# Attention's products of weights and values: fp32 products of 65 columns, or fp32r products of split operands, 130 and 66 columns wide

## The chip, the cores and the metric

The kernel runs on one core of one Trainium2 chip. The time is that of the device from the start to the end of one execution, in microseconds (us); lower is better. The core has five engines that run on their own and meet at semaphores: TensorE (PE in the rows; its weight loads are listed as PEld), VectorE (DVE), ScalarE (ACT), GpSimd (POOL) and SyncE (SP), which here only issues DMAs.

## The reference, cut to what matters

One decoder layer over 1024 tokens of width 1024, all in float32: a projection, two groups of attention heads, an output projection, a mixture of experts, a gated input embedding and a final norm. The change lies in attention alone. Group A has 8 heads with three branches each (keys of all earlier tokens, keys of the last 512 tokens, and 63 compressed keys), group B has 8 heads with a cumulative forget gate in the logits. Since there are just 16 blocks of 64 keys and 16 are selected, the selected branch is plain causal attention.

```python
def _masked_softmax(logits, mask):
    l = jnp.where(mask, logits.astype(jnp.float32), NEG_INF)
    return jax.nn.softmax(l, axis=-1) * mask
...
    # _nsa_mixer, for each block of 64 queries: three branches
    s_c = jnp.einsum('bqghd,bngd->bghqn', qg, kc) * scale
    p_c = _masked_softmax(s_c, cmp_end[None, :] <= t[:, None])
    o_c = jnp.einsum('bghqn,bngd->bqghd', p_c.astype(vc.dtype), vc)
    ...
    o_s = jnp.einsum('bghqk,bgqkd->bqghd', p_s.astype(v_sel.dtype), v_sel)
    ...
    o_w = jnp.einsum('bghqk,bkgd->bqghd', p_w.astype(v_w.dtype), v_w)
    o = gt[..., 0:1] * o_c + gt[..., 1:2] * o_s + gt[..., 2:3] * o_w
...
    # _fox_mixer, for each block of 128 queries
    logits = (jnp.einsum('bqhd,bkhd->bhqk', qb, k).astype(jnp.float32) * scale
              + (cq[..., None] - cum[:, :, None, :]))
    p = _masked_softmax(logits, kpos[None, :] <= t[:, None])
    o = jnp.einsum('bhqk,bkhd->bqhd', p.astype(v.dtype), v)
```

## The kernel before

The stages run one after another, each in a scope of its own: `stage_project`, `stage_compress`, `stage_attention`, `stage_mix`, `stage_route`, `stage_moe`, `stage_finish`. Only `stage_attention` (from L764) is touched.

Work in attention is cut into **units**: a head, a branch (CAUSAL, NEAR, BLOCKS or, for the forgetting heads, FOX) and a half of the queries (four tiles of 128). A unit's blocks of 128 x 128 scores are packed into **banks** of at most 512 columns (`BANKS`). An ordinary head has 20 banks (3 and 7 of CAUSAL, 3 and 5 of NEAR, 1 and 1 of BLOCKS), a forgetting head 10 (3 and 7). That makes 16 heads, 64 units and 240 banks, of which 200 are 512 columns wide and 40 are 256. The banks hold 8 x (36 + 30 + 8) + 8 x 36 = 880 blocks of 128 x 128, and each block takes one product of weights and values.

Scores are computed with the keys on the PSUM partitions, so that a block of exponentials can serve as the stationary operand of the product with the values. The softmax's shift must then be a row of the query operand. It is found ahead: for each head, `minimum` on TensorE computes the scores again, with the queries on the partitions (19 tiles of 512 columns for an ordinary head, 9 for a forgetting one), VectorE reduces each (L1223, L1227), `join` merges halves, `turn` transposes the result, ScalarE copies it (`rows_out`, L1170), and a DMA (L901) writes it into rows of `q_two`. PSUM has `MX` = 4 places for these tiles; a place is free again when VectorE has taken its tile (`ring_before`). `share` spreads the minima of head i + 1 over the banks of head i: over the first 15 of the 20 banks of an ordinary head whose successor is ordinary, over the first 5 of the 10 of a forgetting head (two in each of four banks, one in the fifth).

TensorE's order is a loop over banks b: the scores of bank b + 1 (`score`, L1085, L1096 and the masks L1105), the minima that fall to this bank (L1041, masks L1052), perhaps the turns (L1064), then `weigh(b)` (L1123). The values have a column of ones, so a product has 65 columns and the sum of the weights comes out as the 65th. Both operands of `weigh` are fp32; the other products of attention are fp32r, on operands split into a rounded part and a rest. ScalarE follows with one exponential for each bank (`exps`, L1178) into one of `PT` = 3 buffers. VectorE's order for bank b is its minima, then `leave(u)` if a unit ended with bank b - 1: a reciprocal of the sums (L1248), a product with the gate (L1252, ordinary heads), one with a constant for BLOCKS (L1255), and the output times that (L1259, or L1264 into `tmp` which GpSimd adds, L981). The output of a unit is in one PSUM bank of two, so the first product of unit u waits for `o_made`, that is for `leave(u - 2)`:

```python
                    pe.wait_ge(expd, b + 1)
                    if first_of_unit and u >= 2:
                        pe.wait_ge(o_made, u - 1)
...
                    for kb, qa, qb, at in parts:
                        for q in range(qa, qb):
```

GpSimd makes the rests of the queries and keys (L937, L947) and the additions. SyncE's queue holds the loads of a head, the copies of its rounded halves (`second`) and the row of minima (`rows`).

## Time and profile before

| | us |
|---|---|
| Three runs | 1594.08, 1595.18, 1598.6 (median 1595.18) |
| The profiled execution | 1597.06, of which the span from the first to the last instruction is 1595.4 |
| Attention's stretch, TensorE dense in it | 382.5 to 798 |
| Busy in the span | TensorE 1397.2, VectorE 760.9, ScalarE 629.0, GpSimd 148.5 |
| Mean granted TensorE clock | 0.941 |

The profile gives, for one execution, every instruction with its start and its length. A product's length covers its way through the engine, and products overlap; what one costs in a dense stretch is the distance from one start to the next. Of n equal instructions merged into one row, that distance is the row's length less that of one, divided by n - 1. The granted clock is 1.00 for 2.4 GHz and 0.50 for 1.2 GHz. In a row of windows the columns are the window, its length, busy time with count in brackets for PE, PEld, DVE, ACT and POOL, the granted clock, the DMA engines' share and GB/s.

### The profile page before, as it was taken

The numbers are of one execution on the slowest core, as the hardware profiler recorded it, in microseconds if no ns is written. First come the engines' busy times: TensorE is split into PE (matmuls) and PEld (weight loads), VectorE is DVE, ScalarE is ACT, GpSimd is POOL, SyncE is SP. The second block draws the span as 40 slices with busy tenths as digits, with TensorE's granted clock in tenths as the row PEclk, the third lists the DMA queues.
The fourth block names the chain that finished last, engine by engine and source line by source line (L and its number), as shares of the span: only waits on it lengthen the run. The fifth ranks groups of instructions, "written<-read, shape, count | busy, mean of one in ns | idle before, by whom it ended". The sixth has DMA issues, their size and how long they took to land. (4 is left out here: it accounts for less than half of the span.)

```text
span 1595.4 us, 24135 instructions
## 1 busy us (share of the span) xinstructions
PE 1397.2 (88%) x7996; PEld 1167.6 (73%) x7997; DVE 760.9 (48%) x1240; ACT 629.0 (39%) x930; POOL 148.5 (9%) x146
## 2 busy tenths in 40 slices
PE   4999999737999999999969964999999999628997
PEld 3777889735899989888858854777777777516774
DVE  6633012235444444434254235678654767626552
ACT  6211110013333333445443212567644657515442
POOL 0000000013111112322000000010000000011000
PEclk9999999967999999999979975999999999858999
DMA  5122321144000012354033215799877979464410
GB/s 185 55 75 93 118 75 35 36 104 97 21 21 22 21 46 57 81 125 93 12 121 115 83 53 203 285 331 389 315 253 243 375 259 377 180 237 158 137 49 39
DMA packets 107988, 222.48 MB, mean 139 GB/s; under 512 B 14749, under 2 KB 41405, under 8 KB 107910
## 3 DMA queue, kind: packets, MB, share of 16 engines
q1 hardware_dynamic: 96950, 183.07, 35.4%
q0 software_dynamic: 7488, 27.27, 4.8%
q10 hardware_dynamic: 3472, 11.09, 1.7%
q8 instruction: 50, 0.82, 0.2%
q14 instruction: 28, 0.23, 0.0%
HBM read 176.56 MB, written 36.24 MB: 133 GB/s over the span
## 5 line engine op out<-in xcount | busy, mean ns | idle before, releaser
L1178 ACT ACTIVATE att_prob<-att_ps_s 128x512 f32<-128x512 f32 (+1 forms) x240 | 134.7, 562 | 246.2 <-PE att_ps_s L1105 201.3
L1227 DVE TENSOR_REDUCE att_mx<-att_ps_m 128x1 f32<-128x512 f32 (+3 forms) x256 | 132.8, 560 | 135.0 <-PE att_ps_m L1052 123.2
L1924 DVE TENSOR_TENSOR moe_g_lo<-moe_g_raw,moe_g_hi 128x1024 fp32r<-128x1024 f32 x128 | 148.1, 1218 | 45.5 <-ACT moe_g_hi L1844 44.8
L135 PE MATMUL moe_ps_g<-moe_g_hi,moe_xT_hi 128*128 128x512 f32 x336 | 137.7, 410 | 17.8 <-DVE moe_g_lo L1924 17.7
L1844 ACT ACTIVATE moe_g_hi<-moe_g_raw 128x1024 fp32r<-128x1024 f32 x128 | 124.9, 1047 | 44.4 <-PE moe_ps_g L137 24.4
L1123 PE MATMUL att_ps_o<-tok_vsw,att_prob 128*128 128x65 f32 x1056 | 140.1, 274 | 0.0
L136 PE MATMUL moe_ps_g<-moe_g_lo,moe_xT_hi 128*128 128x512 f32 x336 | 134.3, 400 | 0.0
L137 PE MATMUL moe_ps_g<-moe_g_hi,moe_xT_lo 128*128 128x512 f32 x336 | 133.9, 399 | 0.0
L1123 PEld LDWEIGHTS att_ps_o<-tok_vsw,att_prob 128*128 128x128 f32 x1056 | 131.2, 192 | 2.6 <-ACT att_prob L1178 0.5
L135 PE MATMUL prj_ps_w<-prj_hT_hi,prj_w_hi 128*128 128x512 f32 x256 | 103.0, 402 | 3.0 <-DVE prj_w_lo L405 3.0
L136 PE MATMUL prj_ps_w<-prj_hT_lo,prj_w_hi 128*128 128x512 f32 x256 | 100.3, 392 | 0.0
L137 PE MATMUL prj_ps_w<-prj_hT_hi,prj_w_lo 128*128 128x512 f32 x256 | 100.3, 392 | 0.0
L135 PEld LDWEIGHTS moe_ps_g<-moe_g_hi,moe_xT_hi 128*128 128x128 f32 x336 | 64.0, 190 | 38.4 <-DVE moe_g_lo L1924 21.2
L1929 DVE TENSOR_TENSOR moe_d_lo<-moe_d_raw,moe_d_hi 128x1024 fp32r<-128x1024 f32 x64 | 74.0, 1217 | 23.0 <-ACT moe_d_hi L1850 23.0
L135 PE MATMUL moe_ps_y<-moe_d_hi,moe_hT_hi 128*128 128x512 f32 x168 | 69.2, 412 | 12.0 <-DVE moe_d_lo L1929 12.0
L1123 PE MATMUL att_ps_o<-tok_vb,att_prob 128*128 128x65 f32 x576 | 75.9, 273 | 0.0
L137 PEld LDWEIGHTS moe_ps_g<-moe_g_hi,moe_xT_lo 128*128 128x128 f32 x336 | 64.1, 191 | 15.6
L136 PEld LDWEIGHTS moe_ps_g<-moe_g_lo,moe_xT_hi 128*128 128x128 f32 x336 | 64.2, 191 | 13.8
L1123 PEld LDWEIGHTS att_ps_o<-tok_vb,att_prob 128*128 128x128 f32 x576 | 72.1, 192 | 1.9 <-ACT att_prob L1178 0.2
L338 ACT ACTIVATE att_w_out<-prj_ps_w 128x512 f32<-128x512 f32 x28 | 16.7, 598 | 140.4 <-PE prj_ps_w L137 140.4
L1850 ACT ACTIVATE moe_d_hi<-moe_d_raw 128x1024 fp32r<-128x1024 f32 x64 | 62.4, 1045 | 19.4 <-issue 19.4
L136 PE MATMUL moe_ps_y<-moe_d_lo,moe_hT_hi 128*128 128x512 f32 x168 | 67.1, 399 | 0.0
(339 smaller groups left out, 2909.8 us busy)
## 6 DMA issues: line engine op xcount, KB each, us to landing
moe_g_raw<-in_w_gate_e SPq DMA_DIRECT2D x128, 256.0 KB, 4.9
moe_g_raw<-in_w_up_e SPq DMA_DIRECT2D x128, 256.0 KB, 6.2
moe_d_raw<-in_w_down_e SPq DMA_DIRECT2D x64, 512.0 KB, 7.6
y_rows<-moe_y ACTq DMA_DIRECT2D x21, 512.0 KB, 6.1
prj_w_raw<-in_w_in SPq DMA_DIRECT2D x16, 512.0 KB, 4.0
att_q_raw<-feat SPq DMA_DIRECT2D x32, 256.0 KB
feat<-att_w_out POOLq DMA_DIRECT2D x14, 512.0 KB, 2.9
att_k_raw<-feat SPq DMA_DIRECT2D x24, 256.0 KB
```

Of the source, the lines that this page charges most:

```text
L135: nc.tensor.matmul(out, a_hi, b_hi, start=first, stop=False)
L136: nc.tensor.matmul(out, a_hi, b_lo, start=False, stop=False)
L137: return nc.tensor.matmul(out, a_lo, b_hi, start=False, stop=last)
L338: nc.scalar.activation(out[:, h * 512:(h + 1) * 512], ps_w[:, h, :], ACT.Copy, scale=scale).then_inc(evac, 1)
L1123: last = nc.tensor.matmul(ps_o[:, u % 2, (q % 4) * HV:(q % 4 + 1) * HV], prob[:, b % PT, at + (q - qa) * P:at + (q - qa + 1) * P], value(k ...
L1178: nc.scalar.activation(prob[:, b % PT, 0:w], ps_s[:, b % ST, 0:w], ACT.Exp, scale=-1.0).then_inc(expd, 1)
L1227: last = nc.vector.tensor_reduce(mx[i % 2][:, col, q:q + 1], p[:, at:at + (kb - ka) * P], X, ALU.min)
L1844: nc.scalar.activation(g_hi[:, ch % GR], g_raw[:, ch], ACT.Copy).then_inc(s_ghi, 1)
L1850: nc.scalar.activation(d_hi[:, ch % DR], d_raw[:, ch], ACT.Copy).then_inc(s_dhi, 1)
L1924: nc.vector.tensor_tensor(g_lo[:, ch % GR], g_raw[:, ch], g_hi[:, ch % GR].bitcast(F32), ALU.subtract).then_inc(s_glo, 1)
L1929: nc.vector.tensor_tensor(d_lo[:, ch % DR], d_raw[:, ch], d_hi[:, ch % DR].bitcast(F32), ALU.subtract).then_inc(s_dlo, 1)
```

## The change

The exponentials of a bank are computed twice from PSUM, once rounded to fp32r (`prob_hi`) and once in fp32 (`prob`), and VectorE subtracts the one from the other (`rest`) into `prob_lo`. GpSimd splits the values in the same way into `val`, where the rounded part and the rest of a block of keys lie side by side, 2 x 65 = 130 columns. A block of weights and values is then two fp32r products: `weigh(b, 0)`, the rounded weights times all 130 columns, and `weigh(b, 1)`, the rest of the weights times 66 columns (the rounded values, and one column beside them). The second runs one bank later, behind `weigh(b + 1, 0)`. A unit's output has two sums of 65 columns for each tile of queries and takes two PSUM banks; `leave` first adds the two (a reduction of 512 numbers to 256 into `kc_raw`), and does so one bank later than before. The minima have 2 places in PSUM instead of 4; there are 2 buffers of exponentials instead of 3, one `mT` instead of two, the row of minima goes in two DMAs, and `tmp` lies in `K["cos"]`, whose later load waits for the last addition.

```diff
-        QS, RAW, ST, MX, PT, TM = 3, 2, 2, 4, 3, 2
+        QS, RAW, ST, MX, PR, VR, TM = 3, 2, 2, 2, 2, 3, 2
...
-        prob = sc.sb("prob", [P, PT, 512])
+        prob = sc.sb("prob", [P, PR, 512])
+        prob_hi = sc.sb("prob_hi", [P, PR, 512], F32R)
+        prob_lo = sc.sb("prob_lo", [P, PR, 512], F32R)
+        val = [sc.sb(f"val{s}", [P, NT, 2, HV], F32R) for s in range(VR)]
+        val_c = sc.sb("val_c", [P, GROUPS, 2, HV], F32R)
         mx = [sc.sb(f"mx{s}", [P, 5, NT]) for s in range(2)]
-        mT = [sc.sb(f"mT{s}", [3, S], F32R) for s in range(2)]
+        mT = sc.sb("mT", [3, 2, 512], F32R)
         wt = sc.sb("wt", [P, 2, 4])
-        tmp = sc.sb("tmp", [P, TM, 4, HD])
+        tmp = K["cos"][:, 0:TM * 4 * HD].rearrange("p (a q d) -> p a q d", a=TM, q=4)
         ps_s = sc.ps("ps_s", [P, ST, 512])
         ps_m = sc.ps("ps_m", [P, MX, 512])
-        ps_o = sc.ps("ps_o", [P, 2, 512])
+        ps_o = sc.ps("ps_o", [P, 4, 512])
...
+        sets = [(K["vsw"][:, :, kind * GROUPS + g, :], last_bank(per * (g + 1) - 1, br))
+                for g in range(GROUPS) for kind, br in enumerate((CAUSAL, NEAR))]
+        sets += [(K["vb"][:, :, f, :], last_bank(NH + f, FOX)) for f in range(NH)]
+        def set_of(i, br):
+            return 2 * GROUPS + i - NH if br == FOX else 2 * (i // per) + (br == NEAR)
...
-                    sp.dma_start(q_two[i % QS][R_MIN:R_MIN + rows_of(i), :].bitcast(F32),
-                                 mT[i % 2][0:rows_of(i), :].bitcast(F32)).then_inc(row_in[i % QS], 16)
+                    for half in range(2):
+                        sp.dma_start(q_two[i % QS][R_MIN:R_MIN + rows_of(i), half * 512:(half + 1) * 512].bitcast(F32),
+                                     mT[0:rows_of(i), half, :].bitcast(F32)).then_inc(row_in[i % QS], 16)
...
+                        sp.wait_ge(added, sum(br in (NEAR, BLOCKS) for _, br, _ in units))
...
+                def values(n):
+                    raw, out = sets[n][0], val[n % VR]
+                    if n >= VR:
+                        pool.wait_ge(weighed, sets[n - VR][1] + 1)
+                    nc.gpsimd.tensor_copy(out[:, :, 0, :], raw).then_inc(val_made, 1)
+                    pool.wait_ge(val_made, 2 * n + (3 if n else 1))
+                    nc.gpsimd.tensor_tensor(out[:, :, 1, :], raw, out[:, :, 0, :].bitcast(F32),
+                                            ALU.subtract).then_inc(val_made, 1)
+                    pool.wait_ge(val_made, 2 * n + (4 if n else 2))
...
+                pool.wait_ge(row_set, 4)
+                values(0)
+                block_values()
+                values(1)
...
+                pool.wait_ge(gk_lo, 4)
+                values(2)
                 n = 0
                 for i in range(HEADS):
+                    if i == per:
+                        values(3)
                     if i + 2 < HEADS:
                         q_rest(i + 2)
                         if i + 2 >= NH:
                             k_rest(i + 2 - NH)
+                    if i == per:
+                        values(4)
+                    elif i == NH:
+                        values(5)
+                        values(6)
+                    elif NH < i < HEADS - 2:
+                        values(i - 2)
...
+                def weigh(b, part):
                     u = banks[b][0]
                     i, br, half = units[u]
                     value = operands(i, br)[2]
-                    first_of_unit = b == 0 or banks[b - 1][0] != u
-                    pe.wait_ge(expd, b + 1)
-                    if first_of_unit and u >= 2:
-                        pe.wait_ge(o_made, u - 1)
-                    first, final = first_of_unit, unit_end[u] == b + 1
+                    first = not part and (b == 0 or banks[b - 1][0] != u)
+                    if part:
+                        pe.wait_ge(rest_made, b + 1)
+                    else:
+                        pe.wait_ge(hi_expd, b + 1)
+                        if first:
+                            n = 1 if br == BLOCKS else set_of(i, br)
+                            pe.wait_ge(val_made, 2 * n + (4 if n else 2))
+                            if u >= 2:
+                                pe.wait_ge(o_made, u - 1)
+                            begun.clear()
+                    final = unit_end[u] == b + 1
+                    width = HV + 1 if part else 2 * HV
                     parts = pieces(b)[0]
                     for kb, qa, qb, at in parts:
                         for q in range(qa, qb):
-                            end = final and (kb, q) == (parts[-1][0], qb - 1)
-                            last = nc.tensor.matmul(ps_o[:, u % 2, (q % 4) * HV:(q % 4 + 1) * HV],
-                                                    prob[:, b % PT, at + (q - qa) * P:at + (q - qa + 1) * P], value(kb),
-                                                    start=first, stop=end, skip_group_check=True)
-                            first = False
-                    last.then_inc(weighed, 1)
+                            end = final and part == 1 and (kb, q) == (parts[-1][0], qb - 1)
+                            moving = value(kb, slice(0, 2)).rearrange("p a d -> p (a d)")[:, 0:width]
+                            at_o = (q % 2) * 2 * HV
+                            last = nc.tensor.matmul(ps_o[:, 2 * (u % 2) + q % 4 // 2, at_o:at_o + width],
+                                                    (prob_lo if part else prob_hi)[:, b % PR, at + (q - qa) * P:
+                                                                                   at + (q - qa + 1) * P],
+                                                    moving, start=q % 4 // 2 not in begun, stop=end,
+                                                    skip_group_check=True)
+                            begun.add(q % 4 // 2)
+                    last.then_inc(weighed if part else hi_weighed, 1)
...
-                    weigh(b)
+                    weigh(b, 0)
+                    if b:
+                        weigh(b - 1, 1)
+                weigh(NB - 1, 1)
...
-                    if b >= PT:
-                        act.wait_ge(weighed, b - PT + 1)
-                    nc.scalar.activation(prob[:, b % PT, 0:w], ps_s[:, b % ST, 0:w], ACT.Exp, scale=-1.0).then_inc(expd, 1)
+                    if b >= PR:
+                        act.wait_ge(hi_weighed, b - PR + 1)
+                        act.wait_ge(rest_made, b - PR + 1)
+                    nc.scalar.activation(prob_hi[:, b % PR, 0:w], ps_s[:, b % ST, 0:w], ACT.Exp,
+                                         scale=-1.0).then_inc(hi_expd, 1)
+                    nc.scalar.activation(prob[:, b % PR, 0:w], ps_s[:, b % ST, 0:w], ACT.Exp, scale=-1.0).then_inc(expd, 1)
...
+                def rest(b):
+                    w = pieces(b)[1]
+                    dve.wait_ge(hi_expd, b + 1)
+                    dve.wait_ge(expd, b + 1)
+                    if b >= PR:
+                        dve.wait_ge(weighed, b - PR + 1)
+                    nc.vector.tensor_tensor(prob_lo[:, b % PR, 0:w], prob[:, b % PR, 0:w],
+                                            prob_hi[:, b % PR, 0:w].bitcast(F32), ALU.subtract).then_inc(rest_made, 1)
...
-                    p = ps_o[:, u % 2, 0:4 * HV].rearrange("p (q d) -> p q d", q=4)
+                    both = ps_o[:, 2 * (u % 2):2 * (u % 2) + 2, 0:4 * HV].rearrange("p a (q r d) -> p a q r d", q=2, r=2)
+                    p = K["kc_raw"][:].rearrange("p g (q d) -> p (g q) d", q=2)
                     w = wt[:, u % 2, :]
                     qs = slice(4 * half, 4 * half + 4)
                     dve.wait_ge(weighed, unit_end[u])
-                    own.inc(nc.vector.reciprocal(w, p[:, :, HD]))
+                    own.inc(nc.vector.tensor_reduce(K["kc_raw"][:].rearrange("p g (q d) -> p g q d", q=2),
+                                                    both[:, :, :, :, 0:HD].rearrange("p a q r d -> p a q d r"), X,
+                                                    ALU.add))
+                    own.inc(nc.vector.reciprocal(w.rearrange("p (a q) -> p a q", a=2), both[:, :, :, 0, HD]))
...
+                    rest(b)
+                    if b > 1 and banks[b - 2][0] != banks[b - 1][0]:
+                        leave(banks[b - 2][0])
                     for m in now:
                         minimum(i + 1, m)
                         if m + 1 == len(minima[i + 1]):
                             join(i + 1)
-                    if b and banks[b - 1][0] != banks[b][0]:
-                        leave(banks[b - 1][0])
+                if banks[NB - 2][0] != banks[NB - 1][0]:
+                    leave(banks[NB - 2][0])
```

## Rows read from the trace of the kernel before

**Rows 1.** The page: busy time of each engine, its share, instructions.
```profile
PE 1397.2 (88%) x7996; PEld 1167.6 (73%) x7997; DVE 760.9 (48%) x1240; ACT 629.0 (39%) x930; POOL 148.5 (9%) x146
```

**Rows 2.** Windows: attention in two stretches, and five banks of a forgetting head.
```profile
382.50:668.00 285.50, 285.27 (x2338) 257.53 (x2338) 131.23 (x330) 107.90 (x187) 48.32 (x43) 0.99 0.16 38
668.00:797.00 129.00, 129.00 (x1014) 114.61 (x1013) 53.84 (x124) 61.12 (x105) 30.14 (x14) 1.00 0.33 75
683.73:693.02 9.29, 9.29 (x74) 8.28 (x73) 6.95 (x16) 4.93 (x8) 4.29 (x2) 1.00 0.80 169
```

**Rows 3.** Groups by line, 382.5 to 798 us: busy, mean ns, idle.
```profile
L1123 PE MATMUL att_ps_o<-tok_vsw,att_prob 128*128 128x65 f32 x1056 | 140.1, 274 | 0.0
...
L1178 ACT ACTIVATE att_prob<-att_ps_s 128x512 f32<-128x512 f32 x200 | 119.3, 597 | 204.4 <-PE att_ps_s L1105 159.5 <-PE att_ps_s L1096 43.6
...
L1123 PE MATMUL att_ps_o<-tok_vb,att_prob 128*128 128x65 f32 x576 | 75.9, 273 | 0.0
...
L1123 PE MATMUL att_ps_o<-tok_vc,att_prob 128*128 128x65 f32 x128 | 16.9, 275 | 0.0
```

**Rows 4.** One tile, tok_kc_hi: products on it, shortest, median, longest ns.
```profile
L1041 PEld LDWEIGHTS att_ps_m<-tok_kc_hi,att_q_one x64: 187/191/192, 373.2 to 624.9; 128*128 128x128 f32 x64
L1041 PE MATMUL att_ps_m<-tok_kc_hi,att_q_one x64: 220/274/305, 373.3 to 624.9; 128*128 128x128 f32 x64
```

**Rows 5.** Timeline of weight loads, 479.47 to 479.9 us: start, length, count.
```profile
479.50 0.41 PEld L1041 LDWEIGHTS att_ps_m<-tok_kc_hi,att_q_one 128*128 128x128 f32 x3
```

**Rows 6.** Timeline, 695 to 702 us: four bf16 weight loads.
```profile
701.82 0.27 PEld L1052 LDWEIGHTS att_ps_m<-tok_maskb,tok_identb 128*128 128x128 bf16 x4
```

**Rows 7.** Timeline of TensorE in mixing: 20-column fp32 products.
```profile
871.76 1.96 PE L1524 MATMUL mix_ps_l<-mix_w_rt,mix_uT 128*128 128x20 f32 x16
```

**Rows 8.** Timeline of TensorE in projection: 288-column fp32r products.
```profile
289.78 0.29 PE L135 MATMUL prj_ps_w<-prj_v_hi,prj_hT_hi 128*128 128x288 f32 x1
...
290.98 0.30 PE L135 MATMUL prj_ps_w<-prj_v_hi,prj_hT_hi 128*128 128x288 f32 x1
```

**Rows 9.** Timeline of GpSimd, 345 to 402 us: a subtraction and the wait before.
```profile
365.95 2.36 POOL L937 TENSOR_TENSOR att_q_one<-att_q_raw,att_q_one 64x1024 fp32r<-64x1024 f32 x1 [8.89 <-ACT att_q_one L1156]
```

**Rows 10.** Timeline of TensorE at the end of a head, 488.9 to 495.2 us.
```profile
489.50 0.40 PE L1105 MATMUL att_ps_s<-tok_identb,tok_maskb 128*128 128x128 bf16 x4
...
490.60 0.48 PE L1085 MATMUL att_ps_s<-att_q_one,att_k_one 128*128 128x512 f32 x1
...
491.22 1.06 PE L1123 MATMUL att_ps_o<-tok_vc,att_prob 128*128 128x65 f32 x8
492.09 0.48 PE L1085 MATMUL att_ps_s<-att_q_one,att_k_one 128*128 128x384 f32 x2
...
493.62 1.06 PE L1123 MATMUL att_ps_o<-tok_vsw,att_prob 128*128 128x65 f32 x8
```

**Rows 11.** Timeline of VectorE, 488.9 to 496.5 us.
```profile
489.17 0.18 DVE L1248 RECIPROCAL att_wt<-att_ps_o 128x4 f32<-128x4 f32 x1 [5.62 <-PE att_ps_o L1123]
...
489.59 0.42 DVE L1264 TENSOR_TENSOR att_tmp<-att_ps_o,att_wt 128x256 f32<-128x256 f32 x1
```

**Rows 12.** Groups of VectorE, whole span: a 512-wide subtraction.
```profile
L471 DVE TENSOR_TENSOR prj_v_lo<-att_o,prj_v_hi 128x512 fp32r<-128x512 f32 x8 | 5.0, 686 | 20.2 <-ACT prj_v_hi L372 20.2
```

**Rows 13.** Timeline of VectorE, 683.7 to 693.1 us: two minima back to back.
```profile
687.30 1.28 DVE L1227 TENSOR_REDUCE att_mx<-att_ps_m 128x1 f32<-128x512 f32 x2
```

**Rows 14.** Timeline, 695 to 702 us: the row of minima and who needs it.
```profile
696.76 0.55 SPq L901 DMA_DIRECT2D att_q_two<-att_mT  x1
...
699.85 0.40 PE L1096 MATMUL att_ps_s<-att_q_two,att_k_two 128*128 128x512 f32 x1
```

**Rows 15.** Timeline, 380 to 383 us, at attention's start: the same DMA.
```profile
380.32 0.83 SPq L901 DMA_DIRECT2D att_q_two<-att_mT  x1
...
382.73 0.76 PE L1096 MATMUL att_ps_s<-att_q_two,att_k_two 128*128 128x512 f32 x1 [2.63 <-DMA att_q_two<-att_mT]
```

**Rows 16.** Windows in mixing, just behind the 20-column products, with the granted clock.
```profile
876.00:879.00 3.00, 3.00 (x10) 2.38 (x9) 1.58 (x3) 0.00 (x0) 0.00 (x0) 0.63 0.45 180
```

More of the change, by code:

```diff
@@ L819, in stage_attention, with last_bank @@
         unit_end = [sum(1 for b in range(NB) if banks[b][0] <= u) for u in range(len(units))]
+        def last_bank(i, br):
+            return max(b for b in range(NB) if units[banks[b][0]][:2] == (i, br))
+        per = NH // GROUPS
+        sets = [(K["vsw"][:, :, kind * GROUPS + g, :], last_bank(per * (g + 1) - 1, br))
[3 more added lines that the diff above has]
+            return 2 * GROUPS + i - NH if br == FOX else 2 * (i // per) + (br == NEAR)
         minima = [[(br, n) for br in branches(i) for n in range(len(MINIMA[br]))] for i in range(HEADS)]
@@ L1108, in mask_score @@
                         last.then_inc(scored, 1)
-                def weigh(b):
+                begun = set()
+                def weigh(b, part):
                     u = banks[b][0]
@@ L1167, in rows_out @@
                     act.wait_ge(min_turned, 2 * i + half + 1)
[L1168 to L1170 removed]
+                    if i:
+                        act.wait_ge(row_in[(i - 1) % QS], 32 * ((i - 1) // QS + 1))
+                    nc.scalar.activation(mT[0:rows_of(i), half, :],
                                          ps_m[0:rows_of(i), place(i, f"row{half}"), :], ACT.Copy).then_inc(min_copied, 1)
@@ L1258, in leave @@
                     if br in (CAUSAL, FOX):
-                        nc.vector.tensor_tensor(K["o"][:, qs, i * HD:(i + 1) * HD], p[:, :, 0:HD], wide,
+                        nc.vector.tensor_tensor(K["o"][:, qs, i * HD:(i + 1) * HD], p, wide,
                                                 ALU.mult).then_inc(o_made, 1)
@@ L1263, in leave @@
                         dve.wait_ge(added, parts - TM + 1)
-                    own.inc(nc.vector.tensor_tensor(tmp[:, parts % TM], p[:, :, 0:HD], wide, ALU.mult))
+                    own.inc(nc.vector.tensor_tensor(tmp[:, parts % TM], p, wide, ALU.mult))
                     parts += 1
```

25 lines of the change are left out of this document (15 added, 10 removed).

## The prediction

> **What bounds the kernel now.** I read the page first, then windows over attention, the groups by line there, the waits, and the timelines of three kinds of product. TensorE is busy for 88% of the span [rows 1]. In attention it is busy for 414.3 of 414.5 us at full clock, while VectorE has 185.1 us, ScalarE 169.0 and GpSimd 78.5 [rows 2]. The products of weights and values show no idle time before them [rows 3]. So attention is TensorE's, and the others have room on average. The average hides one thing: during the first five banks of a forgetting head VectorE already has 6.95 us of 9.29 [rows 2].
>
> The records of the products must be counted before they are priced. There are 1056 + 576 + 128 = 1760 [rows 3], but the loops issue 880 products: one fp32 product is two records, each with a weight load. An fp32r product is one record: the 64 products of L1041 on tok_kc_hi (8 heads, 8 tiles of queries) are 64 records [rows 4].
>
> **The products on TensorE.** What does a record cost? In mixing, 16 fp32 records of 20 columns take 1.96 us, the last about 0.27, so (1.96 - 0.27)/15 = 0.113 us from start to start [rows 7]. In attention those of 65 columns run at the same distance: eight take 1.06, the last 0.275, so 0.112 [rows 3, 10]. Columns do not set the price; the load of 128 x 128 four-byte weights does. For fp32r the row is L1041: three successive loads take 0.41 us, the last 0.19, so (0.41 - 0.19)/2 = 0.11 us, with 128 columns streamed [rows 4, 5]. Before: 1760 x 0.112 = 197 us. After: 880 x 2 x 0.112 = 197 us. I take a change of 0. Upper bound: records of 288 columns are (290.98 - 289.78)/9 = 0.133 us apart [rows 8], which on the 880 wide products would be 880 x 0.021 = 18 us. Lower bound: four bf16 loads take 0.27 us in all, 0.067 each at the most [rows 6], which would take away 1760 x 0.045 = 79 us. 130 columns are next to 128, so the row of L1041 is the nearest.
>
> The Trainium skill has a rule that speaks the other way (TensorE: Matmul & The Clock Gate, section "Weight-path perf modes"): the fast weight load is on for 128 weights of any type but FP32. If fp32r counted as another type, the new loads would go at the bf16 distance and the sum would be nearer the lower bound; [rows 5] disagrees, and the trace decides.
>
> **What is added to the other engines.** ScalarE: 200 more exponentials of 512 at 0.597 us [rows 3] and 40 of 256, some 135 us, so 304 of 414; hidden, but each bank now needs 1.2 us before `rest` can start. VectorE: 240 `rest`. A subtraction of 512 lasts 0.686 us [rows 12]. Two reductions of 512 back to back take 1.28 us, so the second starts 1.28 - 0.69 = 0.59 behind the first [rows 13]; I take 0.63 in a queue. That is 200 x 0.63 + 40 x 0.36 = 140 us, and the reduction of 512 in 64 `leave` 64 x 0.60 = 38 us. VectorE rises from 185 to some 363 us of 414. This is below TensorE's sum, but it comes in lumps, and the change takes away the room that lumps need: two places for minima, two buffers of exponentials, and `leave` one bank later. GpSimd: 12 sets of values. A subtraction of 1024 numbers takes it 2.36 us, so one of 520 some 1.2 and the copy no more: 2.4 us a set, 29 us, far ahead of use. The first two sets and the compressed one fall into a wait of 8.9 us for the second query [rows 9]. Price 0; without that cover, 6 us at the start. SyncE's new wait for `added` stands at head 8; behind it are the loads of head 11, the halves of head 10 and the rows of head 9, all needed a head later: 0.
>
> **The chain at the end of an ordinary head.** Two units of one bank follow each other, B0 and B1, then the next head's first bank C0. T0 is the end of B0's bank.
> - Bank B1: its first product needs `leave` of the NEAR unit, whose last products now end at T0. TensorE gets there at T0 + 0.62 (491.22 - 490.60 [rows 10]). The exponentials of B1 start when its masks end (489.90, 0.7 before T0) and take 1.2, so T0 + 0.5. `rest` 0.63. `leave` lasted 489.17 to 490.01, 0.84 [rows 11], and gains 0.60: 1.44. Together T0 + 2.57, a wait of 1.95 us.
> - Bank C0 needs `leave` of B0. With T1 the start of C0's bank, TensorE gets there at T1 + 1.53 (493.62 - 492.09 [rows 10]); VectorE starts `rest` when the last product has drained, T1 + 0.2, then 0.63, then 1.44 and one operation more, for the constant of L1255, which I price as L1252 between 489.35 and 489.59 [rows 11], 0.24: T1 + 2.51, a wait of 0.98.
>
> Together 2.9 us in each of 8 heads: **23 us**.
>
> **The ring of two minima.** A tile in bank b + 1 needs that of two places before taken. I followed both engines' queues bank by bank, with VectorE's order `rest`, `leave`, minima. In an ordinary head (35.3 us) TensorE catches up with VectorE in bank 3 (two minima behind two `leave`: 0.55 us), bank 7 (0.3) and bank 12 (two minima behind a `leave`: 0.7): 1.55 us in 7 heads, **11 us**. In a forgetting head banks 0 to 4 hold nine minima, two `leave` and now five `rest`: VectorE's 6.95 us gain 2.9 + 1.2 = 4.1, 11.0 against TensorE's 9.3 [rows 2]. From the start of bank 0: `rest` from 0.2 to 0.83, the first tile is there at 1.3, two minima of two pieces each (0.68) to 2.66; bank 1, `rest` to 3.3, `leave` (0.67 without a gate, and 0.60) to 4.57, two minima to 5.17 and 5.77. TensorE, at 9.29/5 = 1.86 us a bank, is in bank 2 at 3.7, wants the place of the first of these 0.5 later and gets it at 5.3, the second at 5.9. With the true lengths of the banks it waits 1.4 us in all. Then the row of minima: the DMA is issued at 696.76 and its user starts at 699.85 [rows 14]. At the start of attention, where it was waited for, it took from 380.32 to 382.73 [rows 15], so the slack is 3.1 - 2.4 = 0.7. The copy now stands behind a second exponential (0.6) and the second DMA adds an issue (0.55): late by some 0.65 us. Together 2.05 us in 7 heads, **14 us**. In the last head nothing is made ahead.
>
> **The ends.** Longer `leave` and a last `weigh` part behind a `rest`, a second exponential before bank 0's product, and minima of head 0 through two places: **3 us**.
>
> Sum: 0 + 23 + 11 + 14 + 3 = 51 us. The profiled execution took 1597.06 us, 1.9 above the median, so 1648 there and **1646 us** on the scale of the runs.
>
> **Rivals.**
> - *VectorE's work isn't pipelined so well.* With `rest`, minima and reduction at their full lengths (0.69 and 0.84 instead of 0.60 and 0.68), the same walk gives 7.7 us for an ordinary head and 4.5 for a forgetting one: 58 + 31 + 3 = 92, so 1687 us. For: `rest` follows an instruction on whose semaphore it waits. Against: [rows 13].
> - *The clock falls.* Just behind narrow products and transposes, with TensorE shown busy throughout, the granted clock was 0.63 over 876 to 879 us [rows 7, 16]. The new stretches B1 to C0 have thin products and waits. A stretch of 3.4 us at half clock costs 1.7 us more, one of 10 us costs 5: 14 to 40 us over 8 heads, so 1660 to 1686 us. For: the mixing rows. Against: no wait in the sum is over 2 us, and wide score products stand between them.
> - *Not slower: the delays are absorbed.* VectorE's 363 us lie below TensorE's 414. If `leave` and the minima are taken early enough, only the ends stay: 1595 to 1598 us. It decides only if `leave` is done within 0.6 us of T0, but `rest` and the reduction alone take 1.2. Weak.
> - *Faster: the change does what narrow records would need.* With loads at 0.067 us TensorE's 414 falls to 335, and VectorE's 363 plus its waits for T0 bound the stretch at 363 to 405: 1545 to 1587, say 1575 us. Against: [rows 5]. The Trainium skill's rule above is this case.
>
> **How the numbers follow.** My case 0.57, with a range of its own from 1622 to 1672 (18 for the wide products, half of the ring's sum down); full lengths 0.16; clock 0.16; absorbed 0.05; faster 0.06. The likeliest gives 1646. The range 1608 to 1694 takes in the first three nearly whole and leaves out the last two and an edge above. Within 0.3% is 4.8 us, about what a measurement of this kernel can tell from no change: faster 0.06, same 0.05, slower 0.89.
>
> **What would show it.** 1760 records on prob_hi and prob_lo at 0.11 us; idle time of TensorE in attention of some 50 us, released by att_o or att_tmp (23), att_mx (22) and the DMA of att_mT (4); VectorE at 360 us. The prediction is wrong if records of prob are 0.07 or 0.13 us apart, if the clock in attention is below 0.97, or if TensorE waits for prob_lo or val, which I price at nothing.

## The result, and the profile after

The changed kernel takes 1828.1 us, the median of four runs (1822.17 to 1832.46); the kernel before, measured again beside it, 1595.48. The ratio is 1.145, with a 95% interval from 1.141 to 1.150: 233 us slower. The forecast was 1646 us with a range up to 1694.

In the profiled execution the span goes from 1595.4 to 1822.4 us, 227 more. The first dense score product comes at 390.6 instead of 382.7 us (7.9 later), attention then takes 636.9 instead of 415.1 (221.8 more), and what follows takes 794.9 instead of 797.6. So nearly all of it lies in attention. Two lines of the page, the busy times and the granted clock in 40 slices:

```profile
PE 1597.7 (88%) x7996; PEld 1330.4 (73%) x7997; DVE 969.1 (53%) x1544; ACT 739.1 (41%) x1170; POOL 176.8 (10%) x172
...
PEclk9999999669988755555655799869999999976999
```

Against [rows 1] TensorE has the same number of products, 7996, the same share of the span, 88%, and 200 us more busy time. Equal work that takes longer points at the clock, and the slices from the 15th to the 22nd show fives and one six. Next, windows over attention as a whole, an early ordinary head, a late one, and a forgetting head:

```profile
390.60:1027.50 636.90, 605.05 (x3355) 528.49 (x3355) 392.74 (x757) 278.87 (x532) 98.83 (x75) 0.69 0.14 33
433.17:476.01 42.84, 38.37 (x299) 33.76 (x298) 33.93 (x69) 22.21 (x43) 5.41 (x5) 0.96 0.09 20
611.14:676.74 65.60, 63.54 (x298) 57.04 (x298) 33.55 (x69) 22.43 (x43) 5.43 (x5) 0.55 0.10 22
893.96:924.76 30.80, 29.30 (x134) 24.36 (x134) 17.25 (x29) 12.83 (x25) 6.96 (x4) 0.61 0.29 68
```

The granted clock over attention is 0.69, where it was 0.99 and 1.00 [rows 2]. Two ordinary heads with the same 298 or 299 products take 42.8 us at 0.96 and 65.6 at 0.55; VectorE's busy time is nearly the same in both. The groups by line, in attention:

```profile
L1191 PE MATMUL att_ps_o<-att_val,att_prob_hi 128*128 128x130 f32 x816 | 178.0, 351 | 2.6 <-DVEq L1358 2.1 <-ACT att_prob_hi L1252 0.5
L1191 PE MATMUL att_ps_o<-att_val,att_prob_lo 128*128 128x66 f32 x816 | 161.2, 326 | 0.0
...
L1315 DVE TENSOR_TENSOR att_prob_lo<-att_prob,att_prob_hi 128x512 fp32r<-128x512 f32 x200 | 154.9, 774 | 174.0 <-PE att_ps_o L1191 135.9 <-ACT att_prob L1254 37.4
```

With 64 + 64 more on the compressed values these are 1760 records, as counted ahead. Their lengths rose from 274 ns [rows 3] to 351 and 326; below, 61% of attention turns out to be at half clock. The subtractions take 774 ns in the mean, where 686 were known [rows 12]; that will matter below. The waits of TensorE in attention (us in total, times, longest):

```profile
PEld att_ps_m L1095 <- DVE att_mx L1303: 26.2, 35, 1.6
...
PE att_ps_o L1191 <- DVEq L1358: 17.9, 10, 2.1
...
PE att_ps_m L1095 <- DVE att_mx L1303: 13.0, 18, 1.1
...
PE att_ps_s L1150 <- DMA att_q_two<-att_mT: 3.1, 1, 3.1
```

The releasers are those that the prediction named: the places of the minima, and `leave`. The row of minima is waited for once, at the start. Last, windows cut where the granted clock changes (the stretches between them, at full clock, are left out but for one, and of those at half clock three: 58.0 us from 675.6, and 23.9 each from 904.3 and 935.0):

```profile
433.20:436.60 3.40, 3.40 (x19) 3.21 (x19) 2.67 (x8) 0.83 (x2) 0.69 (x1) 0.51 0.02 5
...
481.00:487.80 6.80, 6.80 (x26) 6.03 (x25) 6.17 (x11) 3.33 (x6) 3.23 (x2) 0.50 0.18 39
487.80:518.60 30.80, 28.02 (x234) 24.71 (x232) 23.29 (x48) 17.46 (x34) 0.73 (x1) 1.00 0.08 18
518.60:532.30 13.70, 13.58 (x57) 12.49 (x58) 8.14 (x20) 4.39 (x9) 4.71 (x4) 0.50 0.10 21
...
566.40:576.60 10.20, 9.26 (x40) 8.14 (x38) 7.43 (x18) 4.09 (x8) 4.96 (x5) 0.50 0.13 27
...
610.70:668.70 58.00, 58.00 (x258) 52.44 (x257) 30.19 (x62) 19.10 (x37) 4.70 (x4) 0.50 0.04 8
...
740.40:859.90 119.50, 117.57 (x493) 102.36 (x493) 64.78 (x119) 46.50 (x86) 28.01 (x21) 0.50 0.19 47
...
873.60:897.50 23.90, 23.85 (x104) 20.73 (x103) 10.39 (x19) 8.20 (x17) 3.37 (x3) 0.50 0.26 68
...
965.70:1010.10 44.40, 44.40 (x183) 37.78 (x184) 22.30 (x42) 15.82 (x31) 3.65 (x3) 0.50 0.01 3
```

Seven falls lie at the end of an ordinary head or in the first six microseconds of the next one (481.0 is the latest, 5 us into it). Four more, at 873.6, 904.3, 935.0 and 965.7 us, lie some 10 us into a forgetting head, behind the waits for the places of minima. In the 4 us before each of the eleven falls TensorE was idle for 1.2 to 2.1 us. What differs is how long the clock stays down: 3.4 us at first, 119.5 later. All stretches of attention at half clock add up to 390.8 us; in the kernel before they were 4.0. If work at half clock takes twice as long, 390.8/2 = 195 us of the 222 are explained, and 27 are left for waits. That is an upper estimate: in `pair66` below, which has no waits, 75.4 us more at half clock made attention 35.1 us longer, 0.47 each, which would give some 180 here. TensorE is shown without any idle time in the 58.0 us from 610.7.

### The profile page after: what moved, and what is told of

Same layout as the page of the kernel before. It is cut to its first block and busy times, and to the rows that moved or that the text cites. A ratio compares the mean times of both kernels' runs of the same rounds, so it can differ in the third digit from the quotient of the medians.

```text
span 1822.4 us, 24977 instructions
## 1 busy us (share of the span) xinstructions
PE 1597.7 (88%) x7996; PEld 1330.4 (73%) x7997; DVE 969.1 (53%) x1544; ACT 739.1 (41%) x1170; POOL 176.8 (10%) x172
## 5 line engine op out<-in xcount | busy, mean ns | idle before, releaser
L1315 DVE TENSOR_TENSOR att_prob_lo<-att_prob,att_prob_hi 128x512 fp32r<-128x512 f32 (+1 forms) x240 | 182.8, 762 | 190.8 <-PE att_ps_o L1191 152.6
L1252 ACT ACTIVATE att_prob_hi<-att_ps_s 128x512 fp32r<-128x512 f32 (+1 forms) x240 | 134.9, 562 | 356.5 <-PE att_ps_s L1159 264.1
L1191 PE MATMUL att_ps_o<-att_val,att_prob_hi 128*128 128x130 f32 x816 | 178.0, 351 | 2.6 <-DVEq L1358 2.1
L1191 PEld LDWEIGHTS att_ps_o<-att_val,att_prob_hi 128*128 128x128 f32 x816 | 161.0, 265 | 10.4 <-ACT att_prob_hi L1252 3.2
L1191 PE MATMUL att_ps_o<-att_val,att_prob_lo 128*128 128x66 f32 x816 | 161.2, 326 | 0.0
L1191 PEld LDWEIGHTS att_ps_o<-att_val,att_prob_lo 128*128 128x128 f32 x816 | 151.9, 258 | 0.1
L1139 PE MATMUL att_ps_s<-att_q_one,att_k_one 128*128 128x512 f32 (+2 forms) x156 | 80.8, 549 | 0.0
```

Source lines behind the costliest of these rows:

```text
L1139: nc.tensor.matmul(out[:, at:at + (qb - qa) * P], one[:, kb * P:(kb + 1) * P], q_one[i % QS][:, qa * P:qb * P], start=first, stop=False, s ...
L1191: last = nc.tensor.matmul(ps_o[:, 2 * (u % 2) + q % 4 // 2, at_o:at_o + width], (prob_lo if part else prob_hi)[:, b % PR, at + (q - qa) * ...
L1252: nc.scalar.activation(prob_hi[:, b % PR, 0:w], ps_s[:, b % ST, 0:w], ACT.Exp, scale=-1.0).then_inc(hi_expd, 1)
L1315: nc.vector.tensor_tensor(prob_lo[:, b % PR, 0:w], prob[:, b % PR, 0:w], prob_hi[:, b % PR, 0:w].bitcast(F32), ALU.subtract).then_inc(rest ...
```

## The experiments

Times are medians; a ratio is to the kernel before, run on the same chip, with its 95% interval. "At half clock" is summed over attention.

### Are the products dearer?

`pair128` and `pair66` put two fp32r products for each block into the kernel before: no rests, no second exponential, four places for minima, three buffers. Beside that only GpSimd copies the values, rounded to fp32r.

```diff
+                            for rep in range(2):
-                            last = nc.tensor.matmul(ps_o[..., (q % 4) * HV:(q % 4 + 1) * HV],
-                                                    prob[...], value(kb), start=first, stop=end, ...)
+                                last = nc.tensor.matmul(ps_o[..., (q % 4) * PW:(q % 4 + 1) * PW],
+                                                        prob[...], moving(value(kb)), start=first, ...)
```

> As pair66, but each of the two fp32r products 128 columns wide (64 columns, and 64 that overlap them): 256 columns for a block, against 260 in the kernel before. It leaves out the rests of weights and values. Theory A: full clock, 1590 to 1600 us. Theory B: the same. Theory C: the clock falls as in pair66, 1700 us or more.

> The kernel before, with its fp32 product of 65 columns replaced by two fp32r products of the same rounded weights with the same rounded values, 66 columns wide: 1760 records again, 132 columns for a block instead of 260. No second exponential, no subtraction, no change of buffers or of VectorE's work. It leaves out the rests of weights and values, and sums the rounded product twice. Theory A: the clock falls though no wait was added, and more than in the changed kernel, 1700 us or more. Theory B: nothing makes TensorE wait, full clock, 1590 to 1600 us. Theory C: the clock falls, 1700 us or more.

`pair128`: 1598.1 us, ratio 1.000 [0.998, 1.003]. `pair66`: 1631.0 us, ratio 1.021 [1.019, 1.023], between the forecasts: neither no change nor 1700 us and more. Windows of `pair128`, then of `pair66` around the return of its clock:

```profile
381.40:796.70 415.30, 415.27 (x3355) 372.88 (x3355) 185.43 (x454) 168.92 (x292) 84.21 (x66) 0.99 0.21 50
...
381.40:385.60 4.20, 4.17 (x20) 3.80 (x20) 0.65 (x2) 1.19 (x2) 0.00 (x0) 0.50 0.43 111
385.60:796.70 411.10, 411.10 (x3337) 369.08 (x3336) 184.79 (x453) 167.72 (x290) 84.21 (x66) 1.00 0.21 49
```

```profile
377.00:382.70 5.70, 2.32 (x10) 1.26 (x10) 0.70 (x1) 2.46 (x3) 1.29 (x2) 0.50 0.06 18
382.70:462.30 79.60, 79.60 (x346) 71.16 (x347) 20.56 (x50) 17.14 (x29) 7.66 (x6) 0.50 0.08 20
462.30:833.10 370.80, 370.80 (x3011) 332.86 (x3010) 165.10 (x405) 152.13 (x263) 76.52 (x60) 1.00 0.22 51
```

So 1760 fp32r records cost what 1760 fp32 records did, and the prediction's term of 0 holds. The Trainium skill's rule on the fast weight load (TensorE: Matmul & The Clock Gate, "Weight-path perf modes") does not extend to these loads. But 66 columns have a price of another kind. The clock was at half before attention began in both kernels; TensorE had little work just then (busy for 2.32 of 5.70 us before 382.7 in `pair66`, 0.57 of 3.40 before 381.4 in `pair128`). With 128 columns it is back after 4.2 us. With 66 it stays down for 79.6 us in which TensorE has no idle time at all, and once it is back it does not fall again in 370.8 us. So narrow products did not make the clock fall here: they kept it from coming back.

### Are width and waits both needed?

`both256` is the changed kernel with both products of a block 256 columns wide: the same 130 columns are read, some of them twice, into columns of PSUM that nobody reads. `lo130` widens the second product alone, from 66 to 130.

```diff
-                    width = HV + 1 if part else 2 * HV
+                    width = 256                 # both256;  lo130: width = 2 * HV
...
-                            at_o = (q % 2) * 2 * HV
+                            at_o = (q % 2) * 256
```

> The changed kernel, with both products of each block 256 columns wide (the 130 columns, and 126 of them again into unused PSUM): the same records and loads, 512 columns for a block, still hidden behind the loads at 0.107 of 0.112 us. Theory A: full clock through attention, the waits of the prediction alone are left, 1640 to 1655 us, and each record at 0.112 to 0.12 us. Theory B and C: 1820 to 1835 us or a little more.

> The changed kernel, with the second product of each block 130 columns wide instead of 66: the same 1760 records and the same weight loads, 260 columns for a block instead of 196; nothing else. Theory A (the clock follows how many columns the products stream): the granted clock in attention comes back towards 1.00 and the time falls to 1640 to 1680 us. Theory B (the clock falls because TensorE now waits for VectorE): the waits are as before, the clock stays low, 1820 to 1835 us. Theory C (fp32r products themselves count for less than fp32 ones): 1820 to 1835 us.

`both256`: 1701.0 us, ratio 1.064 [1.062, 1.067]; 18.5 us at half clock. `lo130`: its runs lie between 1716 and 1754, at mean granted clocks from 0.904 down to 0.888, median 1742.5, too far apart for a ratio; 186 us at half clock in its profile. Both times lie between what width alone (1640 to 1655, 1640 to 1680) and what waits alone (1820 and more) would have given: no forecast fits. More columns, less time. Windows of `both256`: two of its four falls, then an ordinary and a forgetting head at full clock; and the same two heads of the kernel before.

```profile
477.10:480.50 3.40, 3.40 (x17) 3.31 (x16) 1.71 (x5) 0.00 (x0) 0.30 (x1) 0.50 0.00 0
521.50:524.90 3.40, 3.40 (x19) 3.27 (x17) 2.13 (x6) 0.16 (x1) 0.00 (x0) 0.50 0.00 0
...
609.57:653.12 43.55, 38.12 (x298) 33.44 (x297) 33.92 (x69) 22.26 (x43) 5.43 (x5) 1.00 0.13 30
806.02:827.50 21.48, 19.46 (x134) 15.57 (x133) 17.16 (x29) 12.70 (x26) 6.99 (x4) 1.00 0.42 100
```

```profile
527.80:563.54 35.74, 35.74 (x299) 32.35 (x298) 17.25 (x43) 13.21 (x23) 5.31 (x6) 1.00 0.12 26
717.44:734.32 16.88, 16.88 (x135) 14.95 (x134) 7.36 (x17) 8.29 (x15) 4.74 (x2) 1.00 0.54 124
```

The falls are still at the ends of heads, but each lasts 3.4 us, and there are four of them: at the ends of the later ordinary heads TensorE waits as long (1.99 us at 608.5) and the clock stays at 1.00. No forgetting head has a fall. Records at 256 columns are 0.120 us apart, 0.008 more than before, so 148 of them add 1.2 us to an ordinary head and 72 add 0.6 to a forgetting one. That leaves waits of 43.55 - 35.74 - 1.2 = 6.6 us and 21.48 - 16.88 - 0.6 = 4.0 us, where 4.5 and 2.05 were predicted. This kernel is the ruler for the waits, since the clock hardly blurs them.

### Which columns does the clock need?

`wide_start` has 256 columns in the first five banks of each head and thin products (132 and 66) in the others; `wide_rest` is the other way round.

```diff
+                    thin = not ((b - bank_end[i - 1] if i else b) < 5)     # wide_rest: >= 5
+                    width = 256 if not thin else HV + 1 if part else 2 * HV + 2
```

> The changed kernel, with both products of a block 256 columns wide in the first five banks of each head, and thin (132 and 66 columns) in all others. The theory so far (thin products and waits together) is made sharper here: the waits at the end of a head bring the clock down, and how soon it comes back depends on the width of what follows. In the changed kernel it fell at 433.2, 481.0, 518.6, 566.4 and 610.7 us and stayed down for 3.4, 6.8, 13.7, 10.2 and 58.0 us; with all products 256 wide it fell at the same places of a head and was back after 3.4 us each time. Then wide products just behind the fall are enough: below 100 us at half clock in attention (18.5 with all of them wide, 390.8 with all thin), and 1700 to 1745 us. Rival (the mean width over a head is what counts): most records are thin here, 615 blocks of 880, so the clock would be as bad as with 130 columns or worse: 190 to 390 us at half clock, 1745 to 1825 us.

> The other way round: thin products (132 and 66 columns) in the first five banks of each head, 256 columns in all others. Theory (fall at the end of a head, return by the width of what follows): each head starts at half clock and gets back once the wide banks come, some 10 to 15 us later: 100 to 250 us at half clock in attention, 1730 to 1790 us, so slower than wide_start though two thirds of its records are wide. Rival (mean width): 18 to 100 us at half clock, 1700 to 1730 us, faster than wide_start. Second rival (wide products at the end of a head, before the waits, keep the clock from falling): no falls at the ends of heads at all.

`wide_start`: 1702.7 us, ratio 1.069 [1.064, 1.075]; 59.2 us at half clock. `wide_rest`: 1727.6 us, ratio 1.082 [1.079, 1.085]; 93.8 us. Windows over attention, first of `wide_start`, then of `wide_rest`:

```profile
389.80:905.40 515.60, 465.91 (x3355) 401.08 (x3355) 397.05 (x758) 276.58 (x532) 100.34 (x75) 0.94 0.17 40
```

```profile
387.90:925.90 538.00, 485.64 (x3355) 416.26 (x3355) 395.40 (x757) 276.73 (x532) 100.25 (x75) 0.91 0.16 39
```

With fewer wide records, but right behind the fall, the kernel is 25 us faster than with more of them elsewhere: the place counts, not the mean width. Of the 25 us, 34.6 us less at half clock explain some 17, and 350 blocks fewer with two wide records of 0.008 us more each some 5.6. The expectation for `wide_rest` missed in size: I had 100 to 250 us at half clock and 1730 us or more, and both figures fell into the range of its rival; only the order of the two kernels, which the rival had the other way, came as expected. In the ordinary heads of `wide_rest` the stretches were 3.4 us (one was 6.8, and the last head had 17.1) although thin products filled their first five banks. In the forgetting heads they were 10.2 us once and 6.8 five times, while `wide_start` has no fall in any forgetting head: there the waits lie in the first five banks, among wide products. So thin banks behind a fall do not suffice for a stretch of 58 us; it takes more of them.

### What are the waits made of?

`leave_first` is `both256` with `leave` ahead of `rest` on VectorE. `narrow_rest256` is `both256`, and `narrow_rest` the changed kernel, with a `rest` of 2 columns. `before_two_places` is the kernel before with `MX` = 2 and no other change. `short_gpsimd` is `both256` with short subtractions on GpSimd.

```diff
-                    rest(b)
                     if b > 1 and banks[b - 2][0] != banks[b - 1][0]:
                         leave(banks[b - 2][0])
+                    rest(b)                                   # leave_first
...
-            nc.vector.tensor_tensor(prob_lo[:, b % PR, 0:w], ...
+            nc.vector.tensor_tensor(prob_lo[:, b % PR, 0:2], ...     # narrow_rest256, narrow_rest
...
-                    q = q_one[i % QS][HD:P, :]
+                    q = q_one[i % QS][HD:P, 0:2]                     # short_gpsimd, and the keys
```

> The kernel of both256 (1701 us, clock back in attention), with `leave` put ahead of `rest` in VectorE's order of a bank. Theory of the prediction (a chain at the end of each ordinary head: TensorE waits until `rest` and `leave` are done): the two waits of a head shrink by one `rest` each, 0.7 us, so 8 x 1.4 = 11 us less, 1687 to 1694 us. Rival (TensorE waits there for something else, or gets the time back as a later wait): 1697 to 1705 us.

`leave_first`: 1699.8 us, ratio 1.064 [1.060, 1.068], the same as `both256` and not the 11 us less of the theory. The chain itself behaved as foretold: at full clock bank B1 fell from 3.73 to 3.0 us and C0 from 3.9 to 3.2. But the next three banks took 2.3, 2.6 and up to 4.4 us instead of 1.6, 1.4 and 2.3. TensorE's weight loads now wait for `prob_lo` and `prob_hi`, which they hardly did in `both256` (0.9 and 4.4 us):

```profile
PEld att_ps_o L1192 <- ACT att_prob_hi L1253: 16.5, 16, 1.4
PEld att_ps_o L1192 <- DVE att_prob_lo L1316: 12.1, 12, 1.4
```

The `rest` that was put behind `leave` is late, and the time comes back there.

> The kernel of both256 with `rest` computing 2 columns of each bank; the other columns of prob_lo stay zero, so it leaves out the rest of the weights. All waits, buffers and the double exponentials stay. Theory (what is late is VectorE's queue, and mostly the 240 subtractions): VectorE loses some 140 us, the waits for minima nearly vanish and the chain shrinks by 11 us: 1630 to 1655 us. Rival (two places for minima and two buffers of exponentials make the waits by themselves): 1680 us or more.

`narrow_rest256`: 1659.9 us, ratio 1.039 [1.035, 1.044], 5 us above the theory's range; 41 us less than `both256`, 38 of them in attention (474.3 us), and 4.2 us at half clock instead of 18.5. In `both256` the change costs 1701.0 - 1596.7 = 104 us, of which 14 are wider records and 7 the clock, so 83 are left. Of the 41 us, 7 are clock. So VectorE's subtractions are some 34 of the 83, two fifths; the other three fifths stay with the rest of the change (`leave`, two exponentials, two places, two buffers).

> The changed kernel, columns 130 and 66 as they were, with `rest` computing 2 columns of each bank; it leaves out the rest of the weights. Theory A+B (the clock falls where thin products and waits come together): less time at half clock than the 391 us of the changed kernel but not none, 1680 to 1770 us. Theory B alone (waits): as narrow_rest256, 1630 to 1655 us. Theory A alone (thin products, whatever the waits): half clock as before, 1800 us or more.

`narrow_rest`: runs from 1694 to 1769, at mean granted clocks from 0.900 down to 0.861, median 1746.7; 241 us at half clock in its profile. With some 34 us of waits taken away and the widths left at 130 and 66, the clock is still down for most of what the changed kernel had.

> The kernel before with 2 places for minima instead of 4 and nothing else. Theory: with VectorE at 185 us in attention the ring costs nothing there but 4 to 8 us in the minima of head 0, ahead of attention: 1598 to 1606 us. Rival (the ring itself costs the waits): 1620 us or more.

`before_two_places`: 1611.5 us, ratio 1.010 [1.007, 1.012], above the theory's 1598 to 1606 and below the rival's 1620. Attention starts 5.5 us later and is 8.7 longer, 13.1 us of it at half clock, all at its start. Two places alone cost 11 to 20 us by the interval; ordinary heads behind the first do not change, forgetting ones lose 0.6 us each, where the theory had nothing.

> The changed kernel with both products 256 columns wide, as in both256, and GpSimd's subtractions for the queries of heads 1 to 15 and the keys of forgetting heads 3 to 7 cut to 2 columns: left out are the rests of these queries and keys. In both256, 28 of 240 subtractions of VectorE took over 0.9 us, 50.7 us together where 0.69 each would be 19.3; all of them lie beside a subtraction or a copy of GpSimd, up to 2.6 us long, and both read SBUF alone. The minima, which read PSUM, stayed at 0.68 us beside the same. Theory: a part of the missing waits of TensorE (some 82 measured, 48 predicted) is this. The bank of an ordinary head in which it falls took 3.03 us, and 1.59 before; in a forgetting head 3.57 and 2.05. Then both shrink by some 1 to 1.4 us: 6 x 1.2 + 6 x 1.2, so 10 to 20 us less than both256: 1681 to 1691 us. Rival (two minima behind a full-length subtraction and leave make this wait anyway, and GpSimd is beside it): no change of these banks, 1697 to 1704 us.

`short_gpsimd`: 1676.6 us, ratio 1.050 [1.047, 1.052]; 24 us less than `both256`, more than the 10 to 20 expected, though it has 25.8 us at half clock instead of 18.5. The timeline of `both256` in one bank, VectorE and then GpSimd:

```profile
616.98 0.68 DVE L1304 TENSOR_REDUCE att_mx<-att_ps_m 128x1 f32<-128x512 f32 x1
617.58 2.27 DVE L1316 TENSOR_TENSOR att_prob_lo<-att_prob,att_prob_hi 128x512 fp32r<-128x512 f32 x1
619.77 1.28 DVE L1304 TENSOR_REDUCE att_mx<-att_ps_m 128x1 f32<-128x512 f32 x2
```

```profile
616.80 2.50 POOL L956 TENSOR_TENSOR att_q_one<-att_q_raw,att_q_one 64x1024 fp32r<-64x1024 f32 x1
```

GpSimd's subtraction runs from 616.80 to 619.30. VectorE's, begun in between, ends 0.55 us behind it, after 2.27 us instead of 0.69. The reductions, which read PSUM, keep their 0.68. The Trainium skill states this (SBUF — State Buffer, "Who interferes with whom"): a VectorE instruction with two inputs in SBUF and a GpSimd instruction that reads SBUF exclude each other, and the later one stands still. The trace agrees. The groups of `both256` and of `short_gpsimd`:

```profile
L1316 DVE TENSOR_TENSOR att_prob_lo<-att_prob,att_prob_hi 128x512 fp32r<-128x512 f32 (+1 forms) x240 | 186.9, 781 | 102.8 <-ACT att_prob L1255 59.4 <-PE att_ps_o L1192 41.9 <-DVE att_cos L1357 0.3
```

```profile
L1317 DVE TENSOR_TENSOR att_prob_lo<-att_prob,att_prob_hi 128x512 fp32r<-128x512 f32 (+1 forms) x240 | 164.1, 687 | 104.8 <-ACT att_prob L1256 60.0 <-PE att_ps_o L1193 43.2 <-DVE att_cos L1358 0.3
```

The fifth bank of an ordinary head falls from 3.03 to 1.66 us (1.59 in the kernel before), the fourth of a forgetting head from 3.57 to 1.88 (2.05). In a forgetting head the waits drop from 4.0 to 1.8 us (a head takes 19.26 us), between the 1.4 that the walk through the queues had given and its 2.05 with the row of minima; in an ordinary one from 6.6 to about 5.3.

### What would one product cost?

`single66` and `single128` are `pair66` and `pair128` with `range(1)`.

> The kernel before, but each block takes one fp32r product of rounded weights and rounded values, 66 columns wide: 880 records instead of 1760; no wait is added. Left out: the rests of the weights and of the values. Theory (a record costs its load, 0.112 us, and the clock follows the columns that pass): at full clock attention loses 880 x 0.112 = 98 us, 415 to 317, so about 1498 us. But VectorE's minima and ScalarE's exponentials stay, so some of it comes back as waits of TensorE for minima: 1500 to 1530. If thin products alone made the clock fall, as in pair66 (80 us at half clock), it should fall less here, since a larger part of what is left are wide score products: 1500 to 1540. Rival (waits beside thin products make it fall, as in the changed kernel): over 100 us at half clock, 1550 us or more.

> As single66, but the one product is 128 columns wide (the same 64 columns twice); the same parts are left out. A load is still 128 x 128 four-byte weights, so the record distance stays 0.112 us. Theory: full clock, the same waits as single66: 1500 to 1530, and equal to single66 where the clock doesn't fall there. Rival (waits alone bring the clock down): over 50 us at half clock also here, over 1530.

`single66`: 1512.9 us, ratio 0.947 [0.943, 0.951]; 18.2 us at half clock, 10.2 of them in one fall behind a wait of 1.4 us. `single128`: 1507.5 us, ratio 0.946 [0.941, 0.950]; attention takes 325.7 us, 89.4 less than before, where 880 records at 0.112 are 98. The time of these products is their number of weight loads. These two beat both kernels, at the price of the rests of weights and values.

## Why the prediction was wrong, by its steps

- **The count and price of the records, 0: right.** 1760 records; `pair128` has the ratio 1.000. In the stretch of the changed kernel at full clock eight records still take 0.9 us.
- **The clock: the step that failed.** The sum put it at nothing, and the likeliest case took full clock through attention. The prediction had the mechanism as a rival, with a chance of 0.16 and 14 to 40 us. It priced a fall in each ordinary head at 3.4 to 10 us of half clock, with wide score products between the waits as its argument that the clock would hold. It did not: eleven falls, and stretches that grew to 58 and 119.5 us. The prediction's own sign, a clock below 0.97 in attention, came at 0.69. The argument "no wait in the sum is over 2 us" was about true (the longest wait is 2.1) and did not help. At full clock the changed kernel's attention would take about 512.7 - 14 (wider records) - 9 (half of 18.5) = 490 us; it takes 636.9, so the clock costs some 147 us on top of the waits. Counted the other way, work at half clock costs 180 to 195 us and hides all but some 27 to 40 us of the waits. Both are estimates; either is more than the rest of the loss.
- **The chain at the end of an ordinary head, 2.9 us: right, and a little short.** In `both256` B1 takes 3.73 us instead of 1.49 and C0 3.89 instead of 2.39, so 2.2 + 1.4 = 3.6. The timeline of the changed kernel shows the chain, VectorE and then TensorE:

```profile
516.38 0.69 DVE L1315 TENSOR_TENSOR att_prob_lo<-att_prob,att_prob_hi 128x512 fp32r<-128x512 f32 x1 [0.96 <-ACT att_prob L1254]
516.99 0.68 DVE L1335 TENSOR_REDUCE tok_kc_raw<-att_ps_o 128x256 f32<-128x512 f32 x1
...
518.00 0.42 DVE L1354 TENSOR_TENSOR att_cos<-tok_kc_raw,att_wt 128x256 f32<-128x256 f32 x1
```

```profile
518.72 1.08 PE L1191 MATMUL att_ps_o<-att_val_c,att_prob_hi 128*128 128x130 f32 x4 [2.06 <-DVEq L1358]
```

  Starts 516.38 and 516.99 are 0.61 apart, as the row of two minima had said; the wait is 2.06 us against 1.95. Two microseconds later, at 518.6, the clock falls.
- **The ring of two minima: right in kind, 1.55 and 1.4 us became 3.0 and 4.0.** Bank 12 of an ordinary head cost 1.2 us instead of 0.7, bank 3 0.45 instead of 0.55, bank 7 nothing instead of 0.3. The rest is the one step that the walk did not have: VectorE's subtraction standing still beside GpSimd's, 1.4 us in an ordinary head and 2.2 in a forgetting one. The rival with full lengths forecast 1687 us, closer to the 1701 of `both256`, but for a wrong reason: in a queue the operations do start 0.6 us apart. The wait of 0.65 us for the row of minima did not come; by its own terms it was 0.6 + 0.55 - 0.7 = 0.45.
- **The ends, 3 us: 7.9 at the start.** `before_two_places` shows 5.5 of them from two places alone.
- **GpSimd at nothing: wrong.** Its time was free, its hold on SBUF was not: 24 us.
- **VectorE at 360 us:** it has 392.7 in attention; 26 of the excess are 25 stretched subtractions (43.4 us, where 25 x 0.69 are 17.3). In `both256` there are 28, 50.7 us instead of 19.3.
- **The range:** that the change is slower was forecast and came, but that says little for the walk: 51 us were forecast for the waits, `both256` has 83, and the clock more than doubled that. The edges of the likeliest case, 1622 and 1672, do not follow from the two terms named for them, which give some 1634 and 1664.

What is shown: that narrow products without waits keep a low clock low and do not bring it down (`pair66`), that waits with wide products bring few and short falls (`both256`), that both together bring many and long ones, and that wide products right behind the fall end it soon (`wide_start`). What stays open: why the same wait at the end of a head brought a fall in four heads of `both256` and none in the others, why the same sequence of banks was down for 10.2 us in one head and 58.0 in the next, and why `wide_rest` recovered early in its ordinary heads. The experiments do not give a bound from which the clock returns.

## What to carry to other kernels

Price a change of TensorE's products in two currencies: the time at full clock, and what the new mixture does to the granted clock. Here narrow products cost 2% while the engine never waited (`pair66`); with waits of up to 2 us in their midst the clock cost more than all the waits did, and padding the products behind the waits with columns that nobody reads won back 125 us. When an operation with two inputs in SBUF is put on VectorE, list GpSimd's operations at the same place.

## What was not expected of the hardware

- TensorE without any idle time for 79.6 us, half of its records 66 columns wide, at a granted clock of 0.50 (`pair66`); the same with 128 columns went to full clock after 4.2 us. The Trainium skill (TensorE: Matmul & The Clock Gate, "Part 1: The HAM clock gate") lets the clock follow how busy the engine is; by the busy time in the rows it should have come back soon, and the measurement decides.
- A wider product can be faster: 256 columns instead of 130 and 66 made 1828.1 us into 1701.0.
- A VectorE subtraction of 0.69 us took up to 2.6 beside GpSimd, and one of 2 columns (0.16 us alone) up to 2.3. Those that GpSimd's held to its end ended 0.55 us behind it with 512 columns and 0.02 us with 2: most of the time is set by the other's size.
